# Latent attention scores from two-term F32R products: heads in pairs on two row halves, rotated rows stacked on 96 rows, and VectorE's reciprocal placed behind the next pair's maximum

## The reference

```python
q = (rmsnorm(q_lat, g_q) @ w_uq)            # 8 heads x (64 plain + 32 rotated)
kv = (rmsnorm(kv_lat, g_kv) @ w_ukv)        # 8 heads x (64 plain key + 64 value)
q_pe = apply_rope(q_pe, cos, sin)
k_pe = apply_rope(k_rope[:, :, None, :], cos, sin)      # one for all heads
q = concatenate([q_nope, q_pe]) * (96 ** -0.5)
k = concatenate([k_nope, broadcast_to(k_pe)])
s = einsum('bqhd,bkhd->bhqk', qi, k)        # float32
p = softmax(s);  o = einsum('bhqk,bkhd->bqhd', p, v)
```

## Time and profile before

| what | value |
|---|---|
| median of 3 runs (lowest, highest) | 1580.2 us (1579.61, 1580.29) |
| the profiled execution's own time | 1580.01 us |
| its span in the profile | 1578.2 us |
| mean granted TensorE clock over the span | 0.994 of full speed |
| stage B, first and second group | 21 us each, from about 217 and 963 us |
| stage C, first and second group | 114 us each, from about 238 and 984 us |

### The profile page before, as it was taken

How to read it: one execution, slowest core, us unless ns; L and a number is a source line. 1 busy time by engine, 2 the same in 40 slices (tenths; PEclk the granted TensorE clock), 3 DMA queues, 4 the chain that set the end, 5 groups by cost and what they waited for, 6 DMA issues and landing times.

```text
span 1578.2 us, 19306 instructions
## 1 busy us (share of the span) xinstructions
PE 1529.7 (97%) x7352; PEld 1138.6 (72%) x7352; DVE 873.2 (55%) x1531; ACT 689.2 (44%) x1148; POOL 352.4 (22%) x421
## 2 busy tenths in 40 slices
PE   8899999999999999999999999999999999999996
PEld 5667755668777787887887885566877778787885
DVE  4523136665688445886343334576578843688533
ACT  3223235664533444554544334665353344455333
POOL 0011113332010003674310001343201000366410
PEclk9999999999999999999999999999999999999998
DMA  9478841122422241115234444011242234110421
GB/s 372 150 222 257 273 145 44 44 61 80 134 93 93 91 163 41 40 41 213 94 94 153 134 143 124 31 44 61 93 134 94 81 115 139 41 52 29 173 94 67
DMA packets 68988, 179.53 MB, mean 114 GB/s; under 512 B 20624, under 2 KB 21008, under 8 KB 66848
## 3 DMA queue, kind: packets, MB, share of 16 engines
q1 hardware_dynamic: 68896, 178.29, 34.6%
HBM read 153.59 MB, written 24.67 MB: 113 GB/s over the span
## 4 chain that ended last, share of the span: by engine, by line
PE 83%; DVE 7%; ACT 4%; DMA 2%; issue 2%; POOL 1%; SPq 0%; DVEq 0%; ACTq 0%; POOLq 0%
PE ps L486 20%; PE ps L488 20%; PE ps L487 20%; PE ps L974 3%; PE ps L1023 3%; PE ps L1006 3%; PE ps L294 2%; PE ps L991 2%; PE ps L1473 1%; PE ps L1456 1%; PE ps L905 1%; DMA at<-w_ada 1%; PE ps L1507 1%; PE ps L1296 1%; DVE w_lo L468 1%
## 5 line engine op out<-in xcount | busy, mean ns | idle before, releaser
L468 DVE TENSOR_TENSOR w_lo<-at,w_hi 128x1024 fp32r<-128x1024 f32 x162 | 202.0, 1248 | 388.3 <-ACT w_hi L460 388.2
L460 ACT ACTIVATE w_hi<-at 128x1024 fp32r<-128x1024 f32 x162 | 170.4, 1053 | 122.4 <-PE ps L488 122.3
L486 PE MATMUL ps<-h_e_hi,w_hi 128*128 128x512 f32 x480 | 190.9, 398 | 7.8 <-DVE w_lo L468 7.8
L488 PE MATMUL ps<-h_e_hi,w_lo 128*128 128x512 f32 x480 | 187.0, 390 | 0.0
L487 PE MATMUL ps<-h_e_lo,w_hi 128*128 128x512 f32 x480 | 187.0, 389 | 0.0
L486 PE MATMUL ps<-h_a_hi,w_hi 128*128 128x512 f32 x400 | 160.5, 401 | 3.6 <-DVE h_a_lo L518 3.0
L487 PE MATMUL ps<-h_a_lo,w_hi 128*128 128x512 f32 x400 | 156.8, 392 | 0.0
L488 PE MATMUL ps<-h_a_hi,w_lo 128*128 128x512 f32 x400 | 156.8, 392 | 0.0
L486 PEld LDWEIGHTS ps<-h_e_hi,w_hi 128*128 128x128 f32 x480 | 90.1, 188 | 43.7 <-DVE at L1282 11.7
L1129 POOL TENSOR_SCALAR at<-at,at 128x512 f32<-128x512 f32 x128 | 87.0, 692 | 153.9 <-DVE at L1066 153.9
L488 PEld LDWEIGHTS ps<-h_e_hi,w_lo 128*128 128x128 f32 x480 | 90.1, 188 | 19.3
(11 more groups left out here) (258 smaller groups left out, 2978.8 us busy)
## 6 DMA issues: line engine op xcount, KB each, us to landing
at<-blocks_in SPq DMA_DIRECT2D x162, 512.0 KB, 3.8
at<-w_ada SPq DMA_DIRECT2D x32, 512.0 KB, 4.8
at<-w_ada SPq DMA_DIRECT2D x8, 1024.0 KB, 18.0
z_kept<-at SPq DMA_DIRECT2D x32, 256.0 KB, 2.2
at<-z_kept SPq DMA_DIRECT2D x32, 256.0 KB, 2.8
at<-t_masked SPq DMA_DIRECT2D x16, 448.0 KB, 3.3
at<-xs SPq DMA_DIRECT2D x2, 2048.0 KB, 10.9
sg_kept<-at SPq DMA_DIRECT2D x16, 256.0 KB, 4.6
```

Source lines behind the costliest of these rows:

```text
L460: act.activation(whi[:, n % PAIRS], wring[:, n % SLOTS], ACT.Copy).then_inc(sem("w_hi"), 1)
L468: dve.tensor_tensor(wlo[:, n % PAIRS], wring[:, n % SLOTS], whi[:, n % PAIRS].bitcast(F32), ALU.subtract)\
L486: pe.matmul(o, stationary[0], moving[0], start=first, stop=False)
L488: return pe.matmul(o, stationary[1], moving[0], start=False, stop=final)
```

## The change

- **Plain rows.** A QN result of two heads stays one tile: hi by ScalarE (`qn[0]`), lo by VectorE (`qn[1]`); the same for the keys (`kn`). The plain part of two heads' scores is 3 pairs of F32R products of 64 rows, one head on each row half.
- **Rotated rows.** The rotated parts are summed for four heads at once, split into hi and lo (`qrope`), and 24 transfers of 32 rows each, 12 for heads 0 to 3 (`qr_in0`) and 12 for heads 4 to 7 (`qr_in1`), stack hi, hi, lo of each head on 96 rows (`qr3`); the key is stacked as hi, lo, hi (`kr3`). One F32R product of 96 rows then adds all three terms.
- **Pairing.** A latent step is now two heads and one block of queries, so its values are done in every step (`values_of_pair`, 128 queries each, steps 4 to 19). The neighbourhood steps are as before.
- **Places.** `qr3` lies where `xT` does, so `xT` is loaded whole (2 MB) in both groups, behind the last latent score, and the 8 loads of the second group are gone. The wait for `y_out` moves to the head of `c_sync`.
- **Order on VectorE.** The reciprocal of step i - 1 comes behind the maximum of step i.

```diff
-qcat = chunks(take(8 * T, at=Q0), T)
-kcat = chunks(take(8 * T, at=K0), T)
+qn_hl = take_r("qn_s", 8 * T, at=Q0).rearrange("p (n s t) -> p s n t", s=2, t=T)
+qn = (qn_hl[:, 0], qn_hl[:, 1])
+kn = pair("kn", K0, K0 + 4 * T, n=4)
+qrope = [[take_r(f"qrope_{n}{k}", T, at=at) for k, at in enumerate(homes)]
+     for n, homes in enumerate(((V0 + 6 * T, V0 + 10 * T), (N0 + 16 * T, acc_lo)))]
+qr3 = chunks(take_r("qr3", 8 * T, at=xT_lo), T)
+kr3 = take_r("kr3", T, at=V0 + 9 * T)
...
-        if g and 15 <= b < 15 + DC:
-            if b == 15:
-                sp.wait_ge(sem("y_out"), 16 * DC * g)
-            sp.dma_start(xT[:, b - 15], xs[g, :, b - 15]).then_inc(sem("xT_in"), 16)
...
     for p in range(4):
         act.wait_ge(sem("b_full"), at("b_full", J_QN + p + 1))
-        for e in range(2):
-            act.activation(qcat[0:64, 2 * p + e], b_bank(J_QN + p)[64 * e:64 * e + 64], ACT.Copy, scale=QS)\
-                .then_inc(sem("b_act"), 1)
-    act.wait_ge(sem("b_kpe"), at("b_kpe", 1))
-    for h in range(1, HEADS):
-        act.activation(kcat[64:96, h], kcat[64:96, 0], ACT.Copy).then_inc(sem("b_kpes"), 1)
+        act.activation(qn[0][:, p], b_bank(J_QN + p), ACT.Copy, scale=QS).then_inc(sem("b_act"), 1)
+        if p == 1:
+            act.wait_ge(sem("b_rs"), at("b_rs", 1))
+            for lo in (0, 2 * ROPE):
+                act.activation(kr3[lo:lo + ROPE], t0[0:ROPE, 2], ACT.Copy).then_inc(sem("b_rope_hi"), 1)
+    for k in range(2):
+        act.wait_ge(sem("b_rs"), at("b_rs", 2 + k))
+        act.activation(qrope[0][k], t0[:, k], ACT.Copy).then_inc(sem("b_rope_hi"), 1)
+    for p in range(4):
+        act.wait_ge(sem("b_full"), at("b_full", J_KN + p + 1))
+        act.activation(kn[0][:, p], b_bank(J_KN + p), ACT.Copy).then_inc(sem("b_act"), 1)
     if g == 0:
         act.wait_ge(sem("mod_set"), MOD_SET)
     act.activation(shl[:, :, 0], mod[:, 1, 0:DC, g], ACT.Copy).then_inc(sem("shl"), 1)
...
+    dve.tensor_tensor(t0[0:32, 2], t0[0:32, 2], t1[0:32, 2], ALU.add).then_inc(sem("b_rs"), 1)
+    for p in range(4):
+        dve.wait_ge(sem("b_act"), at("b_act", 2 + p + 1))
+        dve.scalar_tensor_tensor(qn[1][:, p], b_bank(J_QN + p), QS, qn[0][:, p].bitcast(F32), ALU.mult, ALU.subtract)\
+            .then_inc(sem("b_lo"), 1)
+        if p == 2:
+            dve.wait_ge(sem("b_rope_hi"), at("b_rope_hi", 1))
+            dve.tensor_tensor(kr3[ROPE:2 * ROPE], t0[0:ROPE, 2], kr3[0:ROPE].bitcast(F32), ALU.subtract)\
+                .then_inc(sem("b_rope_lo"), 1)
     for k in range(2):
         dve.wait_ge(sem("b_full"), at("b_full", J_QR + k + 1))
         dve.tensor_tensor(t1[:, k], b_bank(J_QR + k), cst("sin"), ALU.mult).then_inc(sem("b_t1"), 1)
-    for h in range(HEADS):
-        k, lo = h // 4, 32 * (h % 4)
         dve.wait_ge(sem("b_t1"), at("b_t1", 2 + k))
         dve.wait_ge(sem("b_t0"), at("b_t0", 2 + k))
-        dve.tensor_tensor(qcat[64:96, h], t0[lo:lo + 32, k], t1[lo:lo + 32, k], ALU.add)\
-            .then_inc(sem("b_qr"), 1)
+        dve.tensor_tensor(t0[:, k], t0[:, k], t1[:, k], ALU.add).then_inc(sem("b_rs"), 1)
+    for k in range(2):
+        dve.wait_ge(sem("b_rope_hi"), at("b_rope_hi", 2 + k + 1))
+        dve.tensor_tensor(qrope[1][k], t0[:, k], qrope[0][k].bitcast(F32), ALU.subtract).then_inc(sem("b_rope_lo"), 1)
     for p in range(4):
-        dve.wait_ge(sem("b_full"), at("b_full", J_KN + p + 1))
-        for e in range(2):
-            dve.tensor_copy(kcat[0:64, 2 * p + e], b_bank(J_KN + p)[64 * e:64 * e + 64])\
-                .then_inc(sem("b_kn"), 1)
+        dve.wait_ge(sem("b_act"), at("b_act", 6 + p + 1))
+        dve.tensor_tensor(kn[1][:, p], b_bank(J_KN + p), kn[0][:, p].bitcast(F32), ALU.subtract).then_inc(sem("b_lo"), 1)
...
         if 8 <= n < 11:
-            pe.wait_ge(sem("b_act"), at("b_act", 2 + 2 * (n - 4 - J_QN + 1)))
+            pe.wait_ge(sem("b_lo"), at("b_lo", n - 4 - J_QN + 1))
...
-    sp.wait_ge(sem("b_qr"), at("b_qr", HEADS))
+    if g:
+        sp.wait_ge(sem("y_out"), 16 * DC * g)
+    for k in range(2):
+        for part in range(3):
+            if part == 0:
+                sp.wait_ge(sem("b_rope_hi"), at("b_rope_hi", 2 + k + 1))
+            if part == 2:
+                sp.wait_ge(sem("b_rope_lo"), at("b_rope_lo", 1 + k + 1))
+            for h in range(4):
+                sp.dma_start(qr3[ROPE * part:ROPE * (part + 1), 4 * k + h].bitcast(F32), qrope[part // 2][k][ROPE * h:ROPE * (h + 1)].bitcast(F32))\
+                    .then_inc(sem(f"qr_in{k}"), 16)
     for c in range(2):
         gate(c)
     sp.wait_ge(sem("b_full"), at("b_full", J_END))
...
         gate(c)
+    sp.wait_ge(sem("c_s"), at("c_s", MLA_END))
+    sp.dma_start(xT, xs[g]).then_inc(sem("xT_in"), 16)
     for h in range(2, HEADS):
         bias(h)
...
     def score_pair(j):
 
-        u, half = attention_pair(j)
+        n, m = divmod(j, TM)
         if j == 0:
-            pe.wait_ge(sem("b_qr"), at("b_qr", HEADS))
-            pe.wait_ge(sem("b_kpes"), at("b_kpes", HEADS - 1))
-            pe.wait_ge(sem("b_act"), at("b_act", 2 + HEADS))
+            pe.wait_ge(sem("b_t1"), at("b_t1", 3))
+            pe.wait_ge(sem("b_rope_hi"), at("b_rope_hi", 2))
+            pe.wait_ge(sem("b_rope_lo"), at("b_rope_lo", 1))
         if j == 1:
-            pe.wait_ge(sem("b_kn"), at("b_kn", 6))
-        if half == 0:
-            pe.wait_ge(sem("b_kn"), at("b_kn", u // 2 * 2 + 2))
+            pe.wait_ge(sem("b_lo"), at("b_lo", 4 + 3))
+        if m == 0:
+            pe.wait_ge(sem("b_lo"), at("b_lo", 4 + n + 1))
         if j >= 2:
             pe.wait_ge(sem("c_exp"), at("c_exp", j - 1))
+        col = m * P
+        for s, (a, b) in enumerate(((0, 0), (0, 1), (1, 0))):
+            for e in range(2):
+                r = 64 * e
+                pe.matmul(ps(s_bank(j) + e), qn[a][r:r + 64, n, col:col + P], kn[b][r:r + 64, n], start=(s == 0), stop=False)
+        if m == 0 and n % 2 == 0:
+            pe.wait_ge(sem(f"qr_in{n // 2}"), at(f"qr_in{n // 2}", 192))
         for e in range(2):
-            m = 2 * half + e
-            last = pe.matmul(ps(s_bank(j) + e), qcat[0:QK, u, m * P:(m + 1) * P], kcat[0:QK, u],
-                             start=True, stop=True)
+            last = pe.matmul(ps(s_bank(j) + e), qr3[0:3 * ROPE, 2 * n + e, col:col + P], kr3[0:3 * ROPE], start=False, stop=True)
         last.then_inc(sem("c_s"), 1)
...
+    def values_of_pair(j):
+
+        n, m = divmod(j, TM)
+        if j == 0:
+            pe.wait_ge(sem("b_v"), at("b_v", TM))
+        if m == 0 and n >= 2:
+            pe.wait_ge(sem("d_tmp"), at("d_tmp", n - 1))
+        pe.wait_ge(sem("c_pa"), at("c_pa", j + 1))
+        for s in range(TM):
+            if s == 2:
+                pe.wait_ge(sem("c_pd"), at("c_pd", j + 1))
+            for e in range(2):
+                col = 2 * P * s + P * e
+                last = pe.matmul(ps(6 + n % 2)[64 * e:64 * e + 64, P * m:P * (m + 1)], vmla[:, s, 2 * n + e],
+                                 PT[j % 4][:, col:col + P], start=(s == 0), stop=(s == TM - 1))
+        last.then_inc(sem("c_pv"), 1)
...
         u, half = attention_pair(j)
         n = u // 2
-        if j == 1:
-            pe.wait_ge(sem("b_v"), at("b_v", TM))
-        if half == 0 and n >= 2:
+        if half == 0:
             pe.wait_ge(sem("d_tmp"), at("d_tmp", n - 1))
-        v = vmla if u < HEADS else nav
         pe.wait_ge(sem("c_pa"), at("c_pa", j + 1))
         for s in range(TM):
             if s == 2:
                 pe.wait_ge(sem("c_pd"), at("c_pd", j + 1))
             for e in range(2):
...
                 out0(pe, 0, k)
-        if i >= LV and i % 2:
+        if LV <= i < MLA_END + LV:
+            values_of_pair(i - LV)
+        elif i >= LV and i % 2:
...
             lo_o(i // 4 - 2)
-        if 1 <= i < HALVES + 1:
-            j = i - 1
-            dve.wait_ge(sem("c_exp"), at("c_exp", j + 1))
-            dve.reciprocal(rinv[:, 2 * j:2 * j + 2], rsum[:, 2 * j:2 * j + 2]).then_inc(sem("c_ri"), 1)
         if i < HALVES:
             u, half = attention_pair(i)
             dve.wait_ge(sem("c_s"), at("c_s", i + 1))
...
+        if 1 <= i < HALVES + 1:
+            j = i - 1
+            dve.wait_ge(sem("c_exp"), at("c_exp", j + 1))
+            dve.reciprocal(rinv[:, 2 * j:2 * j + 2], rsum[:, 2 * j:2 * j + 2]).then_inc(sem("c_ri"), 1)
         if LT <= i < HALVES + LT:
             j = i - LT
             dve.wait_ge(sem("c_t"), at("c_t", 2 * j + 2))
...
```

More of the change, by code:

```diff
@@ L62 @@
 PER_GROUP = dict(
-    a_act=4, a_dve=4, b_act=10, b_full=13, b_kn=8, b_kpe=1, b_kpes=7, b_qr=8, b_t0=3, b_t1=3, b_v=4, b_vf=4, blk_done=81,
+    a_act=4, a_dve=4, b_act=10, b_full=13, b_lo=8, b_rope_hi=4, b_rope_lo=3, b_rs=3, b_t0=3, b_t1=3, b_v=4, b_vf=4, blk_done=81,
     c_exp=32, c_max=32, c_nrm=32, c_pa=32, c_pd=32, c_pv=32, c_ri=32, c_s=32, c_t=64, d_hi=8, d_o=8, d_tmp=8, e_conv=80, e_xc=16,
@@ L67 @@
```

(15 more changed lines are left out.)

## The result

The kernel after takes 1588.26 us (median of 5 runs, 1586.73 to 1589.23), the kernel before in the same rounds 1579.87 (1579.22 to 1580.29): ratio 1.0051, 95% interval 1.004 to 1.0063. It is slower by 8.4 us. The forecast was 1578.1, too near to no change to be told from it, with a range up to 1588; the result lies 0.3 above that range. The profiled execution has a span of 1587.1 against 1578.2, a difference of 8.9.

What follows compares the result with a forecast made beforehand. TensorE, with work in flight for 97% of the span, was taken to bound the kernel. Terms summed to -1.2 and -0.65 us in the two groups, together -1.9 from 1580.0: 1578.1, range 1572.5 to 1588.

Steps and rivals of the forecast that it cites:

- Part 2: First rotated product: TensorE waits for 12 row transfers, issued at 0.40 each and landing at 240.6; the wait costs 2.7 us.
- TensorE's clock falls in the new wait: Rival, chance 0.24: half clock for 3.4 to 6.8 us costs 1.7 to 3.4 in each group struck; 1580 to 1585.
- The bound of 5: Upper bound on the first rotated product's wait, if 768 KB of transfers added 4.1 us behind issuing, less overlap.
- The forecast's -1.9: Net change over both groups: -1.2 us in the first and -0.65 in the second.
- Part 1: Stage B: plain score starts when TensorE is free, at 236.88, saving 1.3 us; the bank waits of `b_tensor` just fit.
- Parts 3 and 4: Latent steps: cheaper scores in steps 0 to 3 save 0.7 us; steps 4 to 15 save 1.2.
- don't run at half the price: Rival, chance 0.14: single values cost more per instruction, +6.3 us a group (1591) or +12 (1602).
- The halves don't run side by side: Rival, chance 0.03: plain products take 6 x 0.23 instead of 3, +0.7 us a step, 1600.
- Part 6: Steps 16 to 19: a values block between turns brings two steps from 6.20 to 5.7 us, -1.0 in all.
- Part 7: Reciprocal behind the maximum: 0.1 us in each of 6 pairs from step 20, +0.6; -0.6 at step 31.
- Part 8: Loads of `xT`: the 2 MB load shares bandwidth with head 2's bias table for 2 us at most; +0.3 taken.

Runs made afterwards that it cites:

- experiment 6: Changed kernel with row transfers ordered by head pairs, plus 16 extra transfers of four sizes behind those of heads 0 to 3: 1577.04 us, ratio 0.9977.
- experiment 2: Changed kernel plus 18 products with unused results on TensorE between the plain rows and the wait: 1582.58 us, ratio 1.0016.
- experiment 5: Changed kernel with row transfers ordered by head pairs, and values of two steps done together on odd steps up to 19: 1573.23 us, ratio 0.9952.
- 11: Changed kernel with head-pair transfers, first latent values early, reciprocal ahead in steps 20 to 30, 2 MB load later, values in twos to step 15: 1568.25 us.
- experiment 4: Changed kernel with only the reciprocal put back ahead of the maximum in all steps: 1589.83 us, ratio 1.0059.
- experiment 10: Kernel before with only the reciprocal moved behind the maximum: 1579.23 us, ratio 0.9996.
- experiment 9: Changed kernel with row transfers ordered by head pairs, and the 2 MB load moved behind the bias table of head 5: 1575.61 us, ratio 0.9972.
- experiment 3: Changed kernel with the first two blocks of latent values moved ahead of the first rotated product: 1579.27 us, ratio 0.9995.
- experiment 1: Changed kernel with row transfers ordered by head pairs, six per pair, TensorE waiting for its own pair's six: 1575.87 us, ratio 0.9972.

## Why the prediction was wrong, point by point

- **Part 2 is the step that failed,** and with it the rival "TensorE's clock falls in the new wait" came true in both groups. What failed is the price of the wait for the first 12 transfers, 2.7 us, because an issue was taken at 0.40; and the forecast had the clock behind it at nothing. The forecast had the twelfth row issued at 237.8 and landed at 240.6, a wait of 2.7. Measured, with 0.82 taken off for the later start: first issue 233.5 (forecast 233.4); eleven more at 0.63, so the twelfth at 240.5; landing 2.04 instead of 2.8, TensorE goes on at 242.6. The wait from the end of the plain products (237.95 + 0.89) is 4.6, and in the second group, where one issue took 1.77, 5.7. Why that one took longer is open. The landing was priced 0.8 too dear, the issuing 2.6 too cheap. The Trainium skill, DMA: Bandwidth & Descriptors, Anatomy of one DMA — SWDGE (gpsimd) path, gives about 2.0 us of fixed cost for transfers that GpSimd issues. The 2.04 measured agrees with it, although SP issues here.
- **Why the issue was mis-sized.** It was taken from two gate loads that went out alone, 0.40 each. The trace of before has a burst, too, five loads near its start, of 512 KB or more each:

```profile
3.14 2.73 SPq L341 DMA_DIRECT2D at<-w_ada  x5
```

  That is 0.55 each. At that price the rows land 1.7 later than forecast (11 x 0.15), and the wait is 4.4. The bound of 5 in part 2 holds the first group's 4.6, but not the second's 5.7, and it was worked out from bandwidth, which is not what mattered: the time goes into SP's issues and not into the bytes (experiment 6). That it holds the first at all is luck.
- **The rival's price.** It had 1.7 to 3.4 a group for a stretch at half clock, and measured 3.1 in the chain of after: 1.69 in the latent values (3.41 for 1.72), 0.69 in the plain products, 0.56 and 0.11 in the rotated ones. In whole runs it is 5.7 for both groups (experiment 2). Its time of 1580 to 1585 was too low because it kept the wait at 2.7. The forecast's -1.9, with 1.9 and 3.0 of longer wait and 2 x 3.1 of clock, makes +9.2; the spans differ by 8.9, of which 0.8 is the start's: the sum closes to about 1 us.
- **Its chance.** Against it stood "dense work stands on both sides of it". That work was there, and the clock fell none the less, after 4.49 and 5.58 us. The earlier trace rows had already shown a fall after 2.98, and the forecast's own wait was 2.7.
- **Part 1** gave 1.1 and 0.5 (forecast 1.3 and 0.75, that is 1.3 less the 0.55 of the second group): the first plain product stands 11.51 behind L855 in both groups, where the first score stood 12.59 and 12.04 behind L849. In the second group the bank waits of `b_tensor` did not just fit: TensorE stood 0.34 for VectorE's lo of a QN result.
- **Parts 3 and 4** were right (no experiment put the old scores back; the trace of after carries this): 1.55 to 1.56 a score, 0.88 a turn, 1.02 for the values, 3.46 a step. So the rival of the single values that "don't run at half the price" is out, and so is "The halves don't run side by side". The prediction looked for its first error in the price of a step; that price was right to 0.01. The changes of mode cost what the rows said; experiment 5 takes one away and gets 0.15 back.
- **Part 6** was right in its number, 5.69 for two steps at 16 to 19 (forecast 5.7), but its cause is only half of what the runs show. The block of values between the turns is needed: experiments 5 and 11 take it away and put it back, 6.21 and 5.69. So is the reciprocal's new place, which the forecast had at nothing in these steps: with the block but the reciprocal ahead of the maximum two steps take 6.11 (experiment 4), with the reciprocal behind but no block 6.19 (experiment 10).
- **Part 7** was right within its bounds for what it names: 6.19 instead of 6.12 to 6.13 for two steps from 20 on, 0.06 to 0.07 where 0.1 was taken, and 0.5 gained at the end (0.6 taken). The 0.4 for two steps at 16 to 19, shown just above, is missing in it; in the sum it stands under part 6.
- **Part 8:** the 0.3 a group is neither seen nor ruled out (experiment 9).

## What to carry to other kernels

Price a burst of transfers by a burst: count the issues ahead of the one that the first reader waits for, each at the queue's own pace, and put the transfers in the order of their readers. A new wait on the busiest engine has a second price, the clock behind it; an order of issues that shortens the wait can take back both, here 12.4 us for one loop turned round. Only when the new wait is gone is it worth looking at what the body of the change saves. A saving seen at one place can need two parts of a change at once, as the 5.69 at steps 16 to 19 did; take out each part alone before you name its cause.

## What the runs showed of the hardware

- The issue of a transfer between SBUF tiles costs SP 0.60 to 0.64 us in a burst, for 32 KB as for 256 KB; its landing 2.0 (32 and 64 KB) to 2.5 (256 KB). The first issue after a pause took 0.48 to 0.54, two gate loads issued alone 0.40 each, and two right behind 24 row transfers 1.08 together. What in a burst makes an issue dearer was not tried.
- TensorE's granted clock fell to half for 6.8 us after idle times of 4.49, 5.58 and, in experiment 3, 1.99 us. In the profiled executions it did not fall after 1.70 (experiment 1), 1.97 (experiment 9) and 2.19 (experiment 5):

```profile
982.44 0.73 PE L1012 MATMUL ps<-kr,qr 96*128 96x512 f32 x2 [2.19 <-DMA qr<-qrope]
...
982.40:989.20 6.80, 6.59 (x24) 3.08 (x24) 2.62 (x3) 4.25 (x8) 0.62 (x1) 1.00 0.41 101
```

  So near 2 us the length of the idle time alone does not decide it; what does stays open. It also differs between executions of one kernel: in experiment 3 the mean granted clock of the 11 executions goes from 0.989 (1582.62 us) to 0.994 (1577.28 us), and before, whose profiled execution has no fall at these waits, has 0.994.
